# Norm joints of a two-layer decoder step: half of a result's scaling by the reciprocal root moves from VectorE to GpSimd

## What is computed

```
def _rmsnorm(x, g):
    xf = x.astype(f32)
    y = xf * lax.rsqrt(jnp.mean(xf * xf, axis=-1, keepdims=True) + NORM_EPS)
    return (y * g).astype(x.dtype)

def _sublayer(x, c, w_ada, b_ada, g_pre, g_post, fn):
    mod = (jax.nn.silu(c) @ w_ada + b_ada)[:, None, :]
    shift, scale, gate = jnp.split(mod, 3, axis=-1)
    h = _rmsnorm(x, g_pre) * (1 + scale) + shift
    y, aux = fn(h)
    return x + gate * _rmsnorm(y, g_post), aux
```

## Time and profile before

| | us |
|---|---|
| median of 3 runs | 2658.27 |
| lowest and highest | 2653.91, 2667.56 |
| profiled execution | 2640.63 |
| its span in the trace | 2638.80 |
| mean granted clock of TensorE | 0.909 |

### The profile page before, as it was taken

One profiled execution on the slowest core, in us unless ns is written; L12 is line 12 of the kernel. 1 busy time (PEld: TensorE's weight loads), 2 busy tenths in 40 slices (PEclk: granted clock), 3 DMA queues, 4 the chain that ended last, 5 costly groups with the idle time before them and its releaser, 6 DMA issues. The chain is left out here.

```text
span 2638.8 us, 63437 instructions
## 1 busy us (share of the span) xinstructions
PE 2265.3 (86%) x26373; PEld 1764.4 (67%) x26373; DVE 1438.9 (55%) x2317; ACT 872.2 (33%) x1577; POOL 341.5 (13%) x434
## 2 busy tenths in 40 slices
PE   6898888888877995799999979997877776999998
PEld 3565777776635883577777757655766655777776
DVE  2436787884563447655423274466666656553323
ACT  2335444441231222333322131165333323333222
POOL 2003233331000000111100000023111110111000
PEclk8899999998967986899999989998777788999999
DMA  7423899995273001223233225443999931332331
GB/s 245 112 77 129 300 385 377 376 392 161 87 257 114 4 3 35 64 65 93 83 88 89 82 86 139 142 136 105 267 283 275 270 90 40 91 92 80 89 89 60
DMA packets 306664, 392.62 MB, mean 149 GB/s; under 512 B 23680, under 2 KB 224714, under 8 KB 306404
## 3 DMA queue, kind: packets, MB, share of 16 engines
q1 hardware_dynamic: 276580, 282.15, 34.9%
q0 software_dynamic: 29824, 106.71, 12.3%
HBM read 378.11 MB, written 10.70 MB: 147 GB/s over the span
## 5 line engine op out<-in xcount | busy, mean ns | idle before, releaser
L836 PE MATMUL bank<-yT,WH 128*128 128x288 f16 x3200 | 531.8, 290 | 45.9 <-DVE yT L690 34.6
L836 PEld LDWEIGHTS bank<-yT,WH 128*128 128x128 f16 x3200 | 314.0, 99 | 144.5 <-issue 48.7
L900 DVE SCALAR_TENSOR_TENSOR WL<-wring,WH 128x1024 f16<-128x1024 f32 x194 | 255.1, 1319 | 258.9 <-ACT WH L880 258.8
L1383 DVE TENSOR_TENSOR KL<-bank,KH 128x512 f16<-128x512 f32 x416 | 280.8, 687 | 171.2 <-ACT KH L1363 158.7
L1363 ACT CAST KH<-bank 128x512 f16<-128x512 f32 x416 | 242.0, 584 | 358.1 <-PE bank L1281 356.7
L836 PE MATMUL bank<-uT,WH 128*128 128x288 f16 x2048 | 337.5, 288 | 10.6 <-DVE WL L900 10.6
L836 PE MATMUL bank<-yT,WL 128*128 128x288 f16 x1600 | 331.1, 289 | 0.0
L880 ACT ACTIVATE WH<-wring 128x1024 f16<-128x1024 f32 x194 | 203.5, 1054 | 265.4 <-PE bank L836 220.9
L836 PEld LDWEIGHTS bank<-uT,WH 128*128 128x128 f16 x2048 | 201.5, 98 | 63.1 <-DVE WL L900 11.2
L836 PE MATMUL bank<-uT,WL 128*128 128x288 f16 x1024 | 210.5, 288 | 0.0
L836 PE MATMUL bank<-hT,WH 128*128 128x288 f16 x960 | 164.0, 295 | 31.7 <-DVE hT L727 21.4
(11 more groups left out here) (457 smaller groups left out, 3959.7 us busy)
## 6 DMA issues: line engine op xcount, KB each, us to landing
wring<-in_ada_w SPq DMA_DIRECT2D x96, 512.0 KB, 4.6
vTd<-in_state_dil_k SPq DMA_DIRECT2D x80, 512.0 KB, 13.0
vslot<-in_state_dil_v POOLq DMA_DIRECT2D x78, 512.0 KB, 12.6
yT<-in_cache_fox_k SPq DMA_DIRECT2D x128, 256.0 KB
krows<-in_cache_fox_k SPq DMA_DIRECT2D x128, 256.0 KB
wring<-in_mlp_up SPq DMA_DIRECT2D x64, 512.0 KB, 4.1
wring<-in_mlp_down SPq DMA_DIRECT2D x64, 512.0 KB, 4.0
wring<-in_ev_w_in SPq DMA_DIRECT2D x26, 512.0 KB, 3.8
```

Source lines behind the costliest of these rows:

```text
L836: last = nc.tensor.matmul(bank[b + h][:, 0:HALF], w[s % 2][:, c, :], x[:, s % parts * KC + c, h * HALF:(h + 1) * HALF], start=(s % parts = ...
L900: nc.vector.scalar_tensor_tensor(WL[s % 2][:, :, :], w[:, :, :], WSCALE, WH[s % 2][:, :, :], ALU.mult, ALU.subtract).then_inc(w_free, 1)
L1383: nc.vector.tensor_tensor(KL[i][:, :], turned[n % NT][:, :], KH[i][:, :], ALU.subtract).then_inc(lo_out, 1)
```

## The change

In every joint GpSimd multiplies chunks 4 to 7 by rstd (the new scale_chunks), behind a wait for the same two reciprocals that VectorE waits for. VectorE multiplies chunks 0 to 3 and makes all eight additions: the first three additions still stand between multiplications, the one of chunk 3 behind them, and those of chunks 4 to 7 wait for GpSimd's semaphore scaled_p. GpSimd does this at the start of its block, ahead of clearing spent semaphores.

```diff
+    OWN = KC // 2
+
+    def add_chunks(dve, scaled, scaled_p, added):
+
+        for k in range(OWN):
+            nc.vector.tensor_tensor(yT[:, k, :], yT[:, k, :], rstd[:, :], ALU.mult).then_inc(scaled, 1)
             if k:
                 dve.wait_ge(scaled, k)
                 nc.vector.tensor_tensor(xT[:, k - 1, :], xT[:, k - 1, :], yT[:, k - 1, :], ALU.add).then_inc(added, 1)
+        for k in range(OWN - 1, KC):
+            if k < OWN:
+                dve.wait_ge(scaled, k + 1)
+            else:
+                dve.wait_ge(scaled_p, k - OWN + 1)
+            nc.vector.tensor_tensor(xT[:, k, :], xT[:, k, :], yT[:, k, :], ALU.add).then_inc(added, 1)
+
+    def scale_chunks(pool, inv_ok, scaled_p):
+
+        pool.wait_ge(inv_ok, 2)
+        for k in range(OWN, KC):
+            nc.gpsimd.tensor_tensor(yT[:, k, :], yT[:, k, :], rstd[:, :], ALU.mult).then_inc(scaled_p, 1)
...
+        def on_pool(pool):
+            if add:
+                scale_chunks(pool, inv1, scaled_p)
+        return {"pe": on_pe, "act": on_act, "dve": on_dve, "pool": on_pool, "ready": ready, "whole": whole_ready}
...
                 @block.gpsimd
                 def _(pool):
+                    if before and "pool" in before:
+                        before["pool"](pool)
                     clear_spent()
...
+                @block.gpsimd
+                def _(pool):
+                    scale_chunks(pool, inv1, scaled_p)
```

More of the change, by code:

```diff
@@ L625, in add_chunks @@
                 nc.vector.tensor_tensor(xT[:, k - 1, :], xT[:, k - 1, :], yT[:, k - 1, :], ALU.add).then_inc(added, 1)
+        for k in range(OWN - 1, KC):
[8 more added lines that the diff above has]
+            nc.gpsimd.tensor_tensor(yT[:, k, :], yT[:, k, :], rstd[:, :], ALU.mult).then_inc(scaled_p, 1)
     def renorm(sub, add, whole=False, root_known=False):
         high, rest = split_views(yT)
-        std1, inv1, scaled, added, squared, sum2, std2, inv2 = (
-            sem(n) for n in ("std1", "inv1", "scaled", "added", "squared", "sum2", "std2", "inv2"))
+        std1, inv1, scaled, scaled_p, added, squared, sum2, std2, inv2 = (
+            sem(n) for n in ("std1", "inv1", "scaled", "scaled_p", "added", "squared", "sum2", "std2", "inv2"))
         smp, high_s, rest_s, u_ok, high_ok, rest_ok, whole_ok = (sem(n) for n in ("smp", "high_s", "rest_s", "u_ok", "high_ok", "rest_ok", "whole_ok"))
@@ L675, in on_dve @@
                 inverse(dve, std1, inv1)
-                add_chunks(dve, scaled, added)
+                add_chunks(dve, scaled, scaled_p, added)
                 dve.wait_ge(added, KC)
@@ L709, in whole_ready @@
             pe.wait_ge(whole_ok, KC)
-        return {"pe": on_pe, "act": on_act, "dve": on_dve, "ready": ready, "whole": whole_ready}
+        def on_pool(pool):
+            if add:
+                scale_chunks(pool, inv1, scaled_p)
+        return {"pe": on_pe, "act": on_act, "dve": on_dve, "pool": on_pool, "ready": ready, "whole": whole_ready}
     def mixed_split():
@@ L2620, in add_and_store @@
     def add_and_store():
-        std1, inv1, scaled, added, turned, row_a, smp_a = (sem(n) for n in ("std1", "inv1", "scaled", "added", "turned", "row_a", "smp_a"))
+        std1, inv1, scaled, scaled_p, added, turned, row_a, smp_a = (
+            sem(n) for n in ("std1", "inv1", "scaled", "scaled_p", "added", "turned", "row_a", "smp_a"))
         with ExitStack() as sc:
```

## The result

| | before | after |
|---|---|---|
| median of the first comparison, us | 2661.55 (4 runs) | 2693.06 (4 runs) |
| lowest and highest | 2653.91, 2667.56 | 2686.43, 2696.68 |
| ratio after / before, 95% interval | | 1.011 [1.008, 1.0139] |
| profiled execution, its span | 2640.63, 2638.80 | 2686.43, 2684.6 |
| mean granted clock | 0.909 | 0.897 |

The change makes the kernel slower, as forecast, but by 31.5 us at the median where 16.7 were forecast, and 2693 lies above the range, which ended at 2685.

A forecast was written before the change was run, and what follows sets the result against it. TensorE's sums, slow at the lower clock, were taken to bound three joints, the additions the last. Three joints at +4.4, +4.4 and +4.9 (13.7) plus 3 for the last gave +16.7 us: median 2675, range 2662 to 2685.

The forecast's parts named there:

- Exclusion by turns: In the joints, VectorE and GpSimd lock each other out and alternate; +16.7 us in all, chance 0.62 (+12 to +21).
- The collision of the earlier trace: Before the change, a VectorE split met a running GpSimd addition and took 2.24 us instead of 1.22, 1.02 late.
- the hand-over times of the earlier trace: A GpSimd operation was taken to let go 0.14 us before its end, blocking 1.26 us; a VectorE one 0.60.
- Rival (1): In the joints, VectorE keeps its turn while it has ready work, GpSimd's products come later: +8.2 us, chance 0.20.
- rival (2): In the joints, GpSimd's four products run in one piece once it has the port: about +18 us, chance 0.11.
- rival (3): In the joints, the two engines don't exclude each other and VectorE's operations stay at 0.75 us: -2 us, chance 0.04.
- TensorE sets the joint: In the first three joints TensorE's sums, not VectorE's additions, are the limit; before, they end at 13.57, after at 18.0.
- the clock step: In the sums TensorE's clock rises from 1.2 to 2.4 GHz after 4.1 to 5.1 us; a chunk takes 2.0, then 1.0.
- Nothing outside the joints: Any difference outside the four joints was one the prediction could not account for; other stretches counted as nothing.
- 4 us of spread: Allowance for the spread of medians in the forecast range, with the three runs lying 13.7 us apart.
- The chance on slower (0.62): Chance that the whole kernel gets slower by more than 0.5%, 13.3 us; within that 0.35, faster 0.03.
- rows 6 to 8: Profile rows before the change: collisions in both directions (1.02 and 0.27 us late), and successive GpSimd operations 0.602 us apart.

The follow-up runs named there:

- late_pool: The changed kernel, but GpSimd begins only when VectorE's own four multiplications are done: median 2657.00 us, ratio 1.0028 to the kernel before.
- c_before: The kernel before, unchanged, measured again: median 2646.28 us, ratio 0.998 to the other runs of the kernel before beside it.
- c_after: The changed kernel, unedited, measured again: median 2664.21 us, ratio 1.0059 to the kernel before.
- c_after2: The changed kernel, unedited, measured a third time on another occasion: median 2666.02 us, ratio 1.0083 to the kernel before.
- c_after3: The changed kernel, unedited, measured once more to pool its ratio: median 2670.86 us, ratio 1.0085 to the kernel before.
- one_product: The changed kernel with one product on GpSimd (the last chunk) and seven on VectorE: median 2652.35 us, ratio 1.0029 to the kernel before.
- pool_write: The kernel before with four GpSimd fills of 128x512 beside VectorE's unchanged list in three joints: none of 48 VectorE operations stretched; no median given.

## Why the prediction was right and wrong

**Exclusion by turns: right.** The collision of the earlier trace rows, one of 26 such, and the hand-over times of the earlier trace rows gave the whole order. In joint 1 the forecast places up to the last addition are met within 0.05 us, and four stretched operations and the hole behind chunk 0 are there. Rival (1), VectorE keeping its turn, predicts a first addition at 2.1, rival (2), one piece, at 7.1, rival (3) operations of 0.75; measured is 4.49 with four of 1.95. That the waiting engine always gets its turn was assumed from 0.07 us between two starts; late_pool shows a start of GpSimd's for which it does not hold.
The Trainium skill (SBUF — State Buffer, "Who interferes with whom") has the case: two-input Vector instructions against GpSimd's reads, not against its writes. The trace agrees on both sides, with 1.16 us beside a copy and 0.75 beside a fill. Its "whole instruction" is a little more than measured: with a 1.40 us operation VectorE lost 1.20.

**TensorE sets the joint: right after the change, half right before it.** In every profile of after VectorE idled before the second reciprocal, 2.1 to 3.8 us. In the kernel before TensorE came last in joints 1 and 2 by 0.36 and 0.34 us only; in joint 3, and in joints 1 and 3 of c_before, VectorE went into the reciprocal without idling. That less work on VectorE would have gained nothing there was argued, and no run relieved VectorE without loading GpSimd.

**The sizes: close, and in part by luck.** I took 18.0 for the end of the sums in all three joints; they ended at 18.49, 17.47 and 17.68 in the first profile, from 17.47 to 19.15 in the four of after. So the three joints cost 13.4 us there where 13.7 was forecast, the last 3.9 for 3, and all four 17.3 to 19.4 instead of 16.7. The term behind this is the clock step. The prediction says that every joint had its rise within 5.1 us of steady work; in joints 1 and 2 of that trace it came after 5.4. In the four profiles of after it came 2.8 to 6.2 us after chunk 1, with the same instructions (c_after's second joint took 23.52 us, the others' 21.8 to 21.9). The errors of single joints partly cancelled.

**Nothing outside the joints, and 4 us of spread: wrong. This is the step that failed.** The prediction set every other stretch to zero and gave 4 us for the spread of medians, which ended the range at 2685. The terms of the joints were not the reason: they came to 17.3 us in that profile. Of the 45.8 us between the two profiled executions 28.5 lie outside the joints, 26.2 of them ahead of every changed instruction, the page stage alone with 24.3. And the medians of one program differ by more than 4 us: 2693.06, 2664.21, 2666.02 and 2670.86 us for the changed kernel, 2661.55, 2650.69, 2648.81, 2647.66 and 2646.28 for the kernel before. Of the first 31.5 us, 17.3 are shown in the joints and 2.3 in the stages between them; the remaining 12 fit the page stage, which was 24.3 us longer in that profile, but only one of those four executions has a trace, so that part is not settled, and why the stage was long stays open. That three of the four medians fall into 2662 to 2685 does not make the 4 us right; the range had its width from the rivals. The chance on slower (0.62) was on the right side; rows 6 to 8 would have carried more.

**Does the change cost anything between the joints?** Not shown. Behind joint 2 the projection takes 186.49 us to the prompt's attention in c_after2, 186.48 in c_after3 and in the first profile of after, 184.74 in c_before, and the attention 83.9 against 82.77. In c_before's 184.7 us stretch the clock is 0.99:

```profile
1554.60:1739.30 184.70, 175.96 (x1430) 129.57 (x1428) 87.70 (x149) 39.01 (x63) 0.00 (x0) 0.99 0.50 147
```

The lower level there sums to 3.4 us in c_before and to 8.4 us in c_after2, and 3.4 against 5.2 in the attention. One could think that a joint 4 us longer shifts what follows against the clock's rises and falls. But one_product, whose joint 2 is 0.9 us longer, has the same 186.49 and 83.90; c_after, whose joint 2 is the longest, has 185.78 and 82.70; and the first profile of before had 183.39 and 83.89. The two MLPs are 1.0 to 1.4 and 0.6 to 0.7 us longer than c_before's, and pool_write's second MLP, with the unchanged lists, is 1.7 us longer. The joints alone are enough for the later ratios.

## What to carry to other kernels

Before moving elementwise work from VectorE to GpSimd, find a row in the trace where a VectorE operation with two inputs in SBUF overlaps a GpSimd operation that reads SBUF: if the later one is stretched by the rest of the other, the move adds GpSimd's whole blocked time (1.20 us here) to save VectorE's (0.67). Where it can't be avoided, start GpSimd only when the operations that others wait for are done: the same four products per joint cost 9.8 us over the four joints instead of 17 to 19. And work out who waits for whom behind the list that gets shorter; here TensorE, at half its clock after idling, set three of four joints after the change, while in the kernel before the two were ready within 0.4 us of each other. Last, compare the same program with itself on other occasions before giving a range: its medians differed by 15 us (before) and 29 us (after).

## What the runs showed of the hardware that I had not expected

- With work queued on both sides the two alternate: 16 times in 16, in each of four profiles of the changed kernel, one VectorE operation and one GpSimd product, 1.87 us per pair. It is not a law: in late_pool VectorE got two operations through although GpSimd's first product had already started, four times in four.
- A GpSimd copy of 128x512 with one input blocks a VectorE operation for only 0.41 us, against 1.20 for the product with two; four fills of the same size block for nothing.
- Filling TensorE's idle time with matmuls of constants held the granted clock at 1.00 through the sums of five of six joints, and gained no time in the whole kernel that can be seen; in the sixth the clock was low for 3.4 us all the same.
- Stages with identical instructions differ by 24 us (reading pages, 333.9 to 358.2) and by 17 us (RWKV and its output projection, 467.1 to 484.3) from one execution to the next. The second goes with the time at TensorE's lower clock, 126 us in the shortest and 164 in the longest. A comparison of four runs each had given 1.011, later ones 1.0059 to 1.0085.
